# Products of constants in TensorE's idle stretches, and another order of the attention's sums and additions

## The reference

```python
def reference(x, p, ...):
    h = x
    for i in range(DEPTH):
        if i < N_A_LAYERS:
            h = h + gated_deltanet(rms_norm(h, a_norm[a]), ...)
        else:
            h = h + dilated_attention(rms_norm(h, b_norm[bl]), b_w_q[bl], b_q_norm[bl], b_w_out[bl], kv_blocks)
        h = h + hierarchical_moe(rms_norm(h, ffn_norm[i]), ...)
        h = h + per_layer_embedding(h, p[i], ple_norm[i], w_ple_gate[i], w_ple_proj[i])
        if i == N_A_LAYERS - 1:
            kv_blocks = shared_dilated_kv(h, kv_norm, w_kv, k_norm)
    return h
```

## Time and profile before

| | us |
|---|---|
| median of 3 runs | 1746.33 |
| lowest, highest | 1742.86, 1749.82 |
| the profiled execution's own time | 1737.88 |
| its span | 1736.1 |

### The profile page before, as it was taken

One profiled execution on the slowest core, in us unless ns is written; L12 is line 12 of the kernel. 1 busy time (PEld: TensorE's weight loads), 2 busy tenths in 40 slices (PEclk: granted clock), 3 DMA queues, 4 the chain that ended last, 5 costly groups with the idle time before them and its releaser, 6 DMA issues. The chain is left out here.

```text
span 1736.1 us, 19921 instructions
## 1 busy us (share of the span) xinstructions
PE 1670.3 (96%) x7360; PEld 802.6 (46%) x7360; DVE 698.5 (40%) x1418; ACT 452.7 (26%) x693; POOL 139.5 (8%) x192
## 2 busy tenths in 40 slices
PE   7999999998999999998999999998999999999898
PEld 4555566644334434343355564554344343434343
DVE  4778555515333434333333103455244333424241
ACT  5667233313101011000034716643110100101020
POOL 0026620001000000000000101100000000000000
PEclk9999999999999999999999999999999999999999
DMA  8122332386999999999981020056999999999940
GB/s 288 52 73 46 122 86 73 116 331 225 428 427 426 427 426 426 429 427 427 419 321 49 1 105 1 1 210 274 397 427 426 426 427 427 428 428 428 427 191 39
DMA packets 87385, 482.07 MB, mean 278 GB/s; under 512 B 22544, under 2 KB 39696, under 8 KB 61200
## 3 DMA queue, kind: packets, MB, share of 16 engines
q1 hardware_dynamic: 82704, 472.65, 67.0%
q0 software_dynamic: 4608, 8.40, 1.3%
HBM read 477.35 MB, written 12.06 MB: 282 GB/s over the span
## 5 line engine op out<-in xcount | busy, mean ns | idle before, releaser
L2094 PE MATMUL bank<-ring,xT 128*64 128x512 f32 x2048 | 462.4, 597 | 26.6 <-DMA ring<-in_w 24.9
L2031 DVE TENSOR_TENSOR H<-H,bank 128x512 f32<-128x512 f32 x240 | 154.0, 683 | 303.7 <-PE bank L2082 303.7
L2094 PEld LDWEIGHTS bank<-ring,xT 128*64 128x64 f32 x2048 | 141.6, 136 | 291.1 <-issue 271.0
L2129 PE MATMUL bank<-ring,sg 128*64 128x512 f32 x1024 | 226.8, 595 | 1.7 <-issue 1.2
L2129 PEld LDWEIGHTS bank<-ring,sg 128*64 128x64 f32 x1024 | 71.6, 137 | 133.3 <-issue 126.5
L658 PE MATMUL bank<-ring,ring 128*128 128x512 f32 x256 | 129.1, 600 | 0.0
L643 PE MATMUL bank<-ring,ring 128*128 128x512 f32 x256 | 112.9, 593 | 0.0
L2182 ACT ACTIVATE sg<-bank 128x512 f32<-128x512 f32 x32 | 19.1, 598 | 352.1 <-PE bank L2105 352.1
L2576 PE MATMUL bank<-ring,ring 128*128 128x512 f32 x256 | 110.5, 592 | 0.0
L2082 PE MATMUL bank<-high,Sb 128*128 128x512 f32 x240 | 106.8, 445 | 0.0
L2021 DVE SCALAR_TENSOR_TENSOR low<-bank,weight_now,high 128x512 fp32r<-128x512 f32 x60 | 45.1, 751 | 146.5 <-ACT high L2193 143.4
(11 more groups left out here) (340 smaller groups left out, 1952.0 us busy)
## 6 DMA issues: line engine op xcount, KB each, us to landing
ring<-in_w SPq DMA_DIRECT2D x188, 2048.0 KB, 32.3
ring<-in_w_heads SPq DMA_DIRECT2D x16, 1024.0 KB, 5.1
ring<-in_w SPq DMA_DIRECT2D x16, 512.0 KB, 22.9
ring<-in_w_ple_gate SPq DMA_DIRECT2D x4, 2048.0 KB, 25.9
ring<-in_w_kv SPq DMA_DIRECT2D x3, 2048.0 KB, 19.8
ring<-in_b_w_q SPq DMA_DIRECT2D x3, 2048.0 KB, 19.7
inverses<-ring SPq DMA_DIRECT2D x16, 256.0 KB, 3.9
ring<-inverses SPq DMA_DIRECT2D x16, 256.0 KB, 3.2
```

The costliest lines, as they stand in the source:

```text
L2031: dve.tensor_tensor(out, out, k.bank[6 + j % 2][:, :], ALU.add).then_inc(s.added, 1)
L2094: last = pe.matmul(out[e * SLOTS:(e + 1) * SLOTS, :], k.xT[:, at, e * SLOTS:(e + 1) * SLOTS], w[:, c, e, :], start=(at == 0), stop=(at == ...
L2129: last = pe.matmul(k.bank[2 + n][e * SLOTS:(e + 1) * SLOTS, :], k.hT[:, c, e * SLOTS:(e + 1) * SLOTS], w[:, e, :], start=(c == 0), stop=(c ...
```

## The change

1. A new function `keep_busy` makes one or two float32 products of 256 columns whose operands are constants (the identity and a slice of the constants). Nobody reads the result. It stands at four places, the latter two in the routing of each layer, so six times in the program: behind the last unit of `delta` (two products, bank 0), behind the last unit of the attention (two, bank 0), behind `first_half` in the routing (one, bank 4) and behind the ranks (two, bank 4). The first three have a wait in front, for the reader of what the bank held.
2. In the attention, TensorE makes `sums(11)` behind `combine(7)`, not ahead of it. The early units alternate between banks 1 and 2, so that unit 2 doesn't wait for the last query's scaling any more, but for the first addition; unit 1 waits for the last query's logarithm (`q.ln`), which is what reads bank 2. `FINAL` is changed to suit.
3. In the attention, VectorE adds early unit u one block later than before, and between the maximum and the division, where before it stood behind the division. Two additions are left behind the loop.

```diff
+def keep_busy(pe, k, out, times=2):
+
+    for _ in range(times):
+        pe.matmul(out[:, 0:2 * P], k.ident, k.consts[:, 0:2 * P], start=True, stop=True)
...
                 last.then_inc(done, 1)
+            pe.wait_ge(added, 1)
+            keep_busy(pe, k, bank[OUT_BANKS[0]])
...
-    FINAL = (SUMS, *SCORES, 0, 1, TURNED, TURNED_NEAR, OUT)
+    FINAL = (0, *SCORES, 1, SUMS, TURNED, TURNED_NEAR, OUT)
...
-        return 1 if u == 0 else u % 2
+        return (1, SUMS)[u % 2]
...
-            elif head == LAST:
-                sums(LAST - 1)
...
                 if unit == 1:
-                    pe.wait_ge(s.added, 1)
-                elif unit == 2:
-                    pe.wait_ge(q.out, LAST)
+                    pe.wait_ge(q.ln, LAST)
                 else:
                     pe.wait_ge(s.added, unit - 1)
                 output(bank[early_bank_of(unit)], unit, (0, 1), 0, 1)
             if b >= 0:
                 combine(b)
+            if head == LAST:
+                sums(LAST - 1)
...
+        pe.wait_ge(s.added, EARLY_UNITS + 1)
+        keep_busy(pe, k, bank[FINAL[0]])
...
+        def add_early(u):
+            add(bank[early_bank_of(u)], u, u + 1)
...
                 peak(b + 1)
+                if b > BEGUN:
+                    add_early(b - BEGUN - 1)
                 normalise(b + 1)
             if b + 4 < LAST - 1:
                 scaled(b + 4)
-            if b >= BEGUN:
-                add(bank[early_bank_of(b - BEGUN)], b - BEGUN, b - BEGUN + 1)
             if b + 2 == LAST - 1:
                 scaled(LAST - 1)
+        for u in range(EARLY_UNITS - 2, EARLY_UNITS):
+            add_early(u)
...
     first_half(pe, k, s, (0, 1, 2))
+    pe.wait_ge(s.gdiff, 1)
+    keep_busy(pe, k, k.bank[4], 1)
     pe.wait_ge(s.chosen, 1)
...
     last.then_inc(s.ranks, 1)
+    keep_busy(pe, k, k.bank[4])
```

## The result

| | before | after |
|---|---|---|
| median (6 runs each), us | 1745.45 | 1735.81 |
| lowest, highest | 1742.86, 1749.84 | 1734.60, 1736.87 |
| the profiled execution's own time | 1737.88 | 1734.97 |

The ratio is 0.9945, with a 95% interval of 0.9929 to 0.9960: 9.6 us less, about 0.55%. The forecast was 1744.1, and its range ended at 1737.5. The two profiled executions, however, differ by only 1737.88 - 1734.97 = 2.91 us, and for these the sum had given 2.2.

What follows compares the result with a forecast made beforehand. The prediction took gap-free transfers in the expert stages as the bound, so time won ahead of them counts whole. Its terms, 0.26 - 1.45 - 1.0 = -2.2 us from the median 1746.33, gave 1744.1, range 1737.5 to 1748.5.

Steps and rivals of the forecast that it cites:

- The sum on the profiled execution: Whole kernel: stage ends 0.26, clock -1.45 and attention -1.0 make -2.2 us.
- Stage ends: Ends of delta rule and attention: products nearly hidden behind VectorE's last addition, costing 0.13 us each, 0.26 in all.
- the meeting counts from TensorE's last product: Both stage ends: transposes start 0.86 us later, clock falls as before; sum +0.7, time 1747.1; chance 0.10.
- The clock: Attention's end: idle stretch shrinks to 1.71 us, full clock holds, transposes take 3.81 us instead of 5.26; gain 1.45.
- the rival of a fall elsewhere: Clock not held, falling at another moment of the transposes or routing: sum -0.7, time 1745.6; chance 0.15.
- Routing: Both waits in each layer's routing: products hidden with 0.26 and 0.27 us to spare; cost 0.
- The attention: New order of sums and additions: 0.60 us from the earlier scaling plus 0.40 at block 15, 1.0 us gained.
- the wait for the weights: Before the attention's first early unit: wait for output weights grows from 0.66 us to between 1 and 1.8; gain 0.
- taken from the median, the forecast is 1744.1: Whole kernel: applies the -2.2 us to the shown runs' median of 1746.33, not the profiled execution's 1737.88.
- a transfer rate 1% lower: Expert stages of both layers: offered as explaining 8.6 us, against the unexplained 8.45 between profiled execution and median.
- more falls than the profile shows: In other runs the clock may fall at five more places, 1.45 us each, 7.3 together: 1736.8; chance 0.15.
- the rival's own places: The five other places for clock falls: the delta rule's end and two waits in each routing; 1.45 us each.

Runs made afterwards that it cites:

- no_jump: The kernel before without layer 1's code for further experts (run zero times with these inputs), its test and jump: 1736.41 us, ratio 0.9948.
- the order alone: The changed kernel without any keep_busy product, leaving only the attention's new order: 1744.93 us, ratio 0.9995.
- tiny_products: The changed kernel with its ten products cut from 256 columns to 2, at the same places: 1737.85 us, ratio 0.9958.
- the products at the ends: The kernel before with keep_busy products at the two stage ends only (delta rule, attention), old attention order: 1746.41 us, ratio 1.0011.
- its companions: Layer 1's code for further experts also removed from the order alone (1736.55 us), the products at the ends (1738.48) and the whole change (1735.65).
- padded_delta: The kernel before with ten products of 2 columns, all behind the delta rule's end: 1741.32 us, ratio 0.9979.
- products in the routing: The kernel before with keep_busy products in the routing's two waits only, in both layers: 1743.84 us, ratio 0.9982.

## Why the prediction was wrong

By its own steps:

- **Stage ends, 0.13 us each.** Measured 0.10 and 0.11. Right. The rival that the meeting counts from TensorE's last product is excluded: the idle stretches became 1.38 and 1.69 us.
- **The clock, -1.45 us.** The transposes went from 5.26 to 3.79: -1.47. The size is right, and the rival of a fall elsewhere is excluded for this execution. The reason isn't: the prediction took the length of the idle stretch for what decides (held at 2.13, fallen at 2.44). The profile of `no_jump`, with no products, has it the other way round at the same two places:

```profile
400.76 5.44 PE L312 MATMUL bank<-consts,H 128*128 128x128 f32 x32 [2.14 <-PEq L2850]
...
1194.93 3.81 PE L312 MATMUL bank<-consts,H 128*128 128x128 f32 x32 [2.43 <-PEq L2850]
```

  Over all profiles with nothing at the place, the transposes at the delta rule's end took 3.81 to 3.83 us in five and 5.44 in one; those at the attention's end 5.26 to 5.44 in six and 3.81 in one. With products of 256 or 512 columns, in six kernels, they took 3.79 to 3.82 at both ends each time. So the products keep the clock there, and without them it is mostly lost at the one end and mostly kept at the other; an idle stretch of one length does either.
- **Routing, 0.** Right by the rows above.
- **The attention, -1.0 us.** Measured -0.95, and the wait for the weights as foretold. The medians can't tell it: the order alone is at 0.9995 (0.9985 to 1.0004), which is -0.9 us with an interval from -2.6 to +0.7.
- **The sum on the profiled execution, -2.2 us.** Measured -2.91. The terms as measured make 0.21 - 1.47 - 0.95 = -2.2; 0.64 of the other 0.7 were there before the first product of constants.
- **"taken from the median, the forecast is 1744.1".** This is the step that failed. It subtracts from the median a sum that was made for an execution 8.45 us below it, and so takes for granted that the change doesn't touch what makes the difference. It did. The difference was one late block of instructions at a jump of which that execution shows 0.53 us, and the change moved that block. The prediction named the 8.45 us as unexplained, and offered a transfer rate 1% lower over the expert stages for them. Nothing shows that: TensorE begins with the last piece of weights at 1646.27 to 1647.20 in the three stalled profiles, and at 1646.47 to 1652.16 in the eleven others. The path of the prediction, transfers that set the pace, is right up to there; the last pair's work behind its weights stands on the chain with TensorE alone, and that is where the stall is.
- **The rival "more falls than the profile shows" (0.15).** It gave 1736.8, close to the 1735.81 measured, but for the wrong reason and from the wrong places. `tiny_products` loses the clock at the attention's end and in the routing and is still at 1737.85, and `no_jump` has no products at all. In the stalled profiles the clock also falls in layer 1's last pair, as the stall's consequence, and that is worth 2.57 us of the 8.2. Falls at the rival's own places do occur in some executions: at the delta rule's end and in layer 0's routing in `no_jump` (windows of 0.76 and 0.68), in layer 1's routing in the products at the ends (0.69). The five kernels with products of 256 columns or more in the routing show none there. What this is worth is too small for the medians here.

What is shown and what is argued: that the 8 us lie at the jump is shown by the chains of both kinds and by `no_jump` and its companions. That it is the fetch of instructions rests on the moment of the instruction packet, which agrees in all ten profiles with the jump, and on the kernels in which more instructions with next to no work bring the gain. How the number of instructions sets the packet's moment isn't shown, and why one binary falls in either heap at 24 instructions was not tried; that the fetch races with the last weights' transfers, which take a share of 0.95 to 1.0 there, is argued only. Open too is the part of 2 us in `padded_delta`, and what the products are worth by themselves beyond the profiled 1.5: with the jump out, the whole change against `no_jump` is 0.9939 against 0.9948, which is less than either interval.

## What to carry to other kernels

When the profiled execution lies well off the median of the others, a sum made on it says nothing of the difference: first find an execution of the other kind (another variant's profile will do), compare the two chains, and only then forecast. An idle stretch with "issue" as its reason at a branch, with the transfer queues full, is a suspect even where the profiled execution shows half a microsecond of it. And before instructions that bring a gain are believed for what they do, run as many of them that do nothing: here (`tiny_products`, 0.9958 against 0.9945) they brought three quarters of it.

## What the runs showed of the hardware

- In layer 1, a jump over code that isn't wanted costs 0.5 us on TensorE when its instructions are there (`no_jump` has 0.0), and 4.9 to 6.3 us when the block comes late, with the transfer queues at a share of 1.0. TensorE goes on 2.6 to 2.8 us behind the packet. The clock then falls to 1.2 GHz, and a matrix that takes 7.09 us takes 9.29 to 9.92: the stall costs 7.2 to 8.2 us in all. The same jump in layer 0 took 0.64 to 0.76 us in all fourteen profiles.
- By its times, the same binary can be in either case from one execution to the next (products in the routing: 1734.9 to 1739.0 and 1743.3 to 1748.7), and code hundreds of microseconds ahead of the jump shifts which is the rule.
- Twenty records of 2 columns took 2.29 us at the delta rule's end (0.11 us each) and 4.43 us at the program's start (0.22 each), so that products with next to no work are not free.
- Products of 256 or 512 columns kept the clock at both stage ends in six profiles of six. Products of 2 columns didn't do so reliably: in `tiny_products` the transposes took 3.80 us at the one end and 5.43 at the other, in `padded_delta` 5.43 behind twenty such records (0.54 in the window from 402 to 404). With nothing at all the clock was kept in some executions and lost in others.
